# Two transformer blocks on one core: a pair's output kept in its own r and split later, the small projections' epilogue as a thread

## The reference

```
h  = rms_norm(x, attn_norm)
z  = h @ w_in                          # 2048 -> 1024 (pool) + 3*1024 (r, k, v) + 288 (rates)
zs = token_shift(z[1024:], mu)
r, k, v       = three parts of zs, 1024 each
zw, za, zg    = the last 288 of zs: 64, 64 and 160
decay         = exp(-exp(-softplus(-(w0 + tanh(zw) @ w_up)) - 0.5))
a             = sigmoid(a0 + za @ a_up)
g             = sigmoid(zg) @ g_up
y             = wkv7_scan(r, decay, k', v, -kk, kk*a)     # 16 heads of 64
y             = group_norm(y)*gn_g + gn_b + sum(r*k'*r_k)*v
rwkv_out      = y * g                                     # 1024
pool_out      = causal_multiscale_pool(z[:1024]) @ pool_w * pool_scale
x = x + concat(pool_out, rwkv_out) @ w_out
x = x + relu(rms_norm(x) @ w_ffn_up)^2 @ w_ffn_down
x = x + sigmoid(rms_norm(x) @ w_ple_gate) * (p @ w_ple_proj)
return rms_norm(x, final_norm)
```

## Time and profile before

| | |
|---|---|
| median of 3 runs | 3063.9 us |
| profiled execution, its own time | 3062.03 us |
| span from first to last instruction | 3060.2 us |
| mean granted TensorE clock | 0.975 of full speed |
| busy: PE, DVE, ACT, POOL | 96%, 63%, 47%, 6% of the span |
| DMA | 482.24 MB, 158 GB/s on average |

### The profile page before, as it was taken

One profiled execution on the slowest core, in us unless ns is written; L12 is line 12 of the kernel. 1 busy time (PEld: TensorE's weight loads), 2 busy tenths in 40 slices (PEclk: granted clock), 3 DMA queues, 4 the chain that ended last, 5 costly groups with the idle time before them and its releaser, 6 DMA issues.

```text
span 3060.2 us, 55785 instructions
## 1 busy us (share of the span) xinstructions
PE 2945.8 (96%) x23624; PEld 2874.8 (94%) x23624; DVE 1940.6 (63%) x2218; ACT 1445.7 (47%) x1815; POOL 192.8 (6%) x166
## 2 busy tenths in 40 slices
PE   7998999999999999999997999988899999999998
PEld 7987989999999999999997999976899999999997
DVE  6467767455666676677666676765656556555565
ACT  5356644444554444444445544543444444444464
POOL 0010011000000000000001020222000000000000
PEclk9998999999999999999999999987999999999999
DMA  6644523665566656655654534310366666666654
GB/s 208 187 120 127 166 72 95 183 185 173 187 179 187 186 177 187 183 177 180 191 182 125 176 110 132 103 57 7 95 187 184 183 183 184 182 185 182 184 169 142
DMA packets 252105, 482.24 MB, mean 158 GB/s; under 512 B 16944, under 2 KB 22320, under 8 KB 251728
## 3 DMA queue, kind: packets, MB, share of 16 engines
q1 hardware_dynamic: 251856, 478.68, 52.6%
HBM read 476.53 MB, written 2.10 MB: 156 GB/s over the span
## 4 chain that ended last, share of the span: by engine, by line
PE 83%; DVE 8%; ACT 5%; DMA 2%; issue 2%; POOL 0%; DVEq 0%; ACTq 0%; SPq 0%
PE psm L411 75%; PE psb L468 7%; DVE slo L325 3%; DVE ar L496 2%; ACT ar L493 2%; ACT shi L315 1%; DVE ar L504 1%; DMA raw<-in_w_in 1%; PE psb L476 0%; DVE x L496 0%; DVE ar L507 0%; ACT L493 0%; DMA raw<-in_w_down 0%; ACT gf L493 0%; DVE gl L504 0%
## 5 line engine op out<-in xcount | busy, mean ns | idle before, releaser
L325 DVE TENSOR_TENSOR slo<-raw,shi 128x1024 fp32r<-128x1024 f32 (+1 forms) x901 | 1125.0, 1254 | 715.8 <-ACT shi L315 713.2
L315 ACT ACTIVATE shi<-raw 128x1024 fp32r<-128x1024 f32 (+1 forms) x901 | 947.0, 1054 | 1174.4 <-PE psm L411 942.5
L411 PE MATMUL psm<-gh,shi 128*128 128x256 f32 x3664 | 1052.1, 287 | 17.1 <-DVE slo L325 14.6
L411 PE MATMUL psm<-gl,shi 128*128 128x256 f32 x3664 | 1040.9, 284 | 0.0
L411 PE MATMUL psm<-gh,slo 128*128 128x256 f32 x3664 | 1040.7, 284 | 0.0
L411 PE MATMUL psm<-hh,shi 128*128 128x256 f32 x3408 | 975.6, 286 | 24.0 <-DVE slo L325 17.0
L411 PE MATMUL psm<-hl,shi 128*128 128x256 f32 x3408 | 968.3, 284 | 0.0
L411 PE MATMUL psm<-hh,slo 128*128 128x256 f32 x3408 | 967.9, 284 | 0.0
L411 PEld LDWEIGHTS psm<-gh,shi 128*128 128x128 f32 x3664 | 706.6, 193 | 24.4 <-DVE slo L325 16.1
L411 PEld LDWEIGHTS psm<-gl,shi 128*128 128x128 f32 x3664 | 706.5, 193 | 1.0 <-issue 0.3
L411 PEld LDWEIGHTS psm<-gh,slo 128*128 128x128 f32 x3664 | 705.9, 193 | 0.3
(11 more groups left out here) (188 smaller groups left out, 1304.9 us busy)
## 6 DMA issues: line engine op xcount, KB each, us to landing
raw<-in_w_in SPq DMA_DIRECT2D x240, 512.0 KB, 3.7
raw<-in_w_up SPq DMA_DIRECT2D x176, 512.0 KB, 4.2
raw<-in_w_ffn_up SPq DMA_DIRECT2D x128, 512.0 KB, 3.8
raw<-in_w_ffn_down SPq DMA_DIRECT2D x128, 512.0 KB, 4.0
raw<-in_w_down SPq DMA_DIRECT2D x88, 512.0 KB, 4.6
raw<-in_w_out SPq DMA_DIRECT2D x64, 512.0 KB, 4.1
raw<-in_w_ple_gate SPq DMA_DIRECT2D x32, 512.0 KB, 4.9
raw<-in_w_branch_b SPq DMA_DIRECT2D x16, 512.0 KB, 3.9
```

The costliest lines, as they stand in the source:

```text
L315: hi_tok[j] = A.do(lambda e: e.activation(shi[:, s, 0:m], raw[:, q, 0:m], ACT.Copy), landed, pe_tok.get(j - NS), chain=False, cost=0.22 + ...
L325: lo_tok[j] = V.do(lambda e: e.tensor_tensor(slo[:, s, 0:m], raw[:, q, 0:m], shi[:, s, 0:m].bitcast(F), ALU.subtract), landed, hi_tok[j], ...
L411: e.matmul(out, l, r, start=st, stop=sp, skip_group_check=True),
```

## The change

First, a pair's output `y` is written over its own r (`zr[:, c, :]`, no longer read by then), `s.te` is set there, and the wait for `rkv_end` with the split into `hh`/`hl` goes into a generator of its own, `give`: put in lane 2 when `rkv_end` isn't there yet, run at once when it is. Second, the lora epilogue becomes a generator `lora` in lane 2 behind `finish`, with `scale_x` behind it; it frees its PSUM slot itself, so `group` now waits at a group's first tile until the slot has been freed, and the `rkv` epilogue waits until `lora` is written out.

```diff
--- before.py
+++ after.py
@@ -424,6 +424,8 @@
             k = 0
             for ti, (w, r, kc, c, n) in enumerate(ts):
                 j = cur[1]
+                if ti == 0:
+                    bg_until(lambda: slot.free is not None)
                 first_toks = (lo_tok[j], *(slot.free if ti == 0 else ()))
                 bg_ready(max(Queue.when(t) for t in first_toks))
                 PE.wait(*first_toks)
@@ -1389,7 +1391,6 @@
                 yield (tv,)
 
         nm1, x_done = nm, []
-        bgs[2].append(scale_x())
 
 
         al = Al()
@@ -1476,23 +1477,32 @@
         z_toks = {}
         l_tok = []
 
-        def epi_lora(ps, tp):
-            fg_drain()
-            need_rb()
+        def lora(ps, tp, slot):
+            while hn[0].rb is None:
+                yield
+            yield (hn[0].rb, tp)
             parts = [(lo_[0:n, i, :], lraw[0:n, i, :], 24 + i, n) for i, n in enumerate((128, 128, 32))]
             for dst, src, c, n in parts:
                 t_free = tt(src, ps[0:n, 256 * (c - 24):256 * (c - 24) + 256], rb[0:n, :], ALU.mult, tp)
+            slot.free = (t_free,)
             for dst, src, c, n in parts:
                 ta = act(dst, src, ACT.Copy, t_free, scale=omu[0:n, c:c + 1])
+            yield (ta,)
             for dst, src, c, n in parts:
                 tv = stt(dst[:, 1:256], src[:, 0:255], W("mu", c, 1)[0:n, :], dst[:, 1:256], ALU.mult, ALU.add, ta)
+            yield (tv,)
             act(lo_[0:64, 0, :], lo_[0:64, 0, :], ACT.Tanh, tv)
             act(lo_[:, 1, :], lo_[:, 1, :], ACT.Tanh, scale=0.5)
             ta = act(lo_[0:32, 2, :], lo_[0:32, 2, :], ACT.Tanh, scale=0.5)
+            yield (ta,)
             ts(lo_[:, 1, :], lo_[:, 1, :], 0.5, 0.5, ALU.mult, ALU.add, ta)
             l_tok.append(ts(lo_[0:32, 2, :], lo_[0:32, 2, :], 0.5, 0.5, ALU.mult, ALU.add))
             l_tok.append(ta)
-            return (t_free,)
+            yield ()
+
+        def epi_lora(ps, tp):
+            fg_drain()
+            bgs[2] += [lora(ps, tp, slots[nb[0] % 2]), scale_x()]
 
         group("lora", act_h, epi_lora)
 
@@ -1511,6 +1521,7 @@
 
             def epi(ps, tp):
                 fg_drain()
+                bg_until(lambda: l_tok)
                 if h:
                     bg_until(lambda: 3 in pooled and 0 in kk_tok)
                 tv = in_rms(rraw, ps, tp, kk_pe.get(0))
@@ -1728,11 +1739,21 @@
             tv = stt(yb, b.ap[:, 0:256], W("gn_g", c, 1), t2, ALU.mult, ALU.mult)
             b.free = (tv,)
             stt(yb, yb, W("gn_b", c, 1), bon, ALU.add, ALU.add)
-            tv = tt(yb, yb, gate_, ALU.mult, t_gate)
+            y = zr[:, c, :]
+            tv = tt(y, yb, gate_, ALU.mult, t_gate)
+            s.te = (tv,)
+            out = give(c, y, tv)
+            if rkv_end:
+                next(out)
+            else:
+                bgs[2].append(out)
+            yield ()
+
+        def give(c, y, tv):
+
             while not rkv_end:
                 yield
-            rw_tok[c] = hilo(hh[:, 8 + c, :], hl[:, 8 + c, :], yb, tv, rkv_end[0])
-            s.te = (rw_tok[c],)
+            rw_tok[c] = hilo(hh[:, 8 + c, :], hl[:, 8 + c, :], y, tv, rkv_end[0])
             yield ()
 
         for h in range(2):
```

## The result

The changed kernel took 3030.1 us (median of 4 runs, 3028.5 to 3033.9), the kernel before 3066.0 us on the same chip (4 runs, 3063.2 to 3069.0): a ratio of 0.988, with a 95% interval of 0.987 to 0.990, some 36 us less. Forecast were 3023 us, with 3006 to 3046 as the range. The profiled execution's span fell from 3060.2 to 3026.7 us, by 33.5 us.

A forecast was written before the change was run, and what follows sets the result against it. TensorE was taken to lose time waiting for a lora split and where the pairs' dependent chains stand alone. From 3062.0 us profiled, 27.5 for the pairs and 13 for lora gave 3021.5; plus 1.9, 3023 us; range 3006 to 3046.

The forecast's parts named there:

- Lora: Lora and first rkv group: TensorE's 9.9 us wait for a split goes, 13 us saved, 9.9 as lower end.
- The last two rkv groups: Stretch taking in pairs 2 and 3 nearly whole: 54 to 97.5 us, 7 of it loss.
- Rival (2): Last two rkv groups: POOL operations hold up DVE's splits, costing 10 us, total 3033; chance 0.08.
- Half 0's out2b: Only starts of pairs 6 and 7 stand beside its groups: 70 to 39 us.
- the loss of 7 us: Half 0's out2b: 7 us taken as lost, since only starts of pairs 6 and 7 stand there.
- Rival (1): Starts keep their price: out2b loses 20 us again, rkv groups 12, total 3041; chance 0.17, worst form 0.03.
- Out2a: Out2a with the rest of pairs 2 and 3, and pairs 4 and 5: 95 to 100 us, 6 lost.
- The tail: From half 0's out2b's fourth group's close to the next group's: 108 to 63 us, bounds 56 and 71.
- 60 - 7 + 2 + 8.7: Tail: old G-to-last-lower-part time, less full-clock saving, plus transposes and scaling, plus next group's close: 63 us.
- the saving of 7 us on G: Tail's beginning: 32 G products take 7 us at full clock instead of 14 at half.
- Rival (3): Pairs' part gives nothing, moved work costing the rkv groups what it saves behind; lora alone, 3051; chance 0.05.
- rival (4): TensorE falls to half clock over the last two rkv groups; at two thirds of it, 3076; chance 0.04.

The follow-up runs named there:

- the first experiment: Kernel before with only the lora epilogue moved to its own thread, pairs unchanged: 3053.6 us, ratio 0.9973.
- the split rows: Changed kernel with half 1's four out2b groups of 512 rows cut in two sets of four, 256 rows each: 3034.4 us, ratio 0.9908.
- the fill: Changed kernel plus 48 weight products whose result nobody reads, behind the G steps of pairs 6 and 7: 3034.6 us, ratio 0.991.
- the pairs' part alone: Kernel before with only the pairs' output written over r, lane released at once and split later, lora as before: 3043.1 us, ratio 0.9933.
- turns: Changed kernel with the G steps of pairs 6 and 7 taking turns: 3032.4 us, ratio 0.9886.
- turns with the split apart: Changed kernel with G steps taking turns and the split of a pair's output always its own step in the third lane: 3034.0 us, ratio 0.989.
- second profile: Changed kernel run again unaltered, as the ruler for the runs beside it: 3031.6 us, ratio 0.9882.

## Why the prediction was right, and where its sizes were off

**Lora.** Right in place and size: 12.1 us for 13, and the first rkv group without the wait. It stands alone in the first experiment, with the same 47 us, though only 8.3 us of it reached that run's total.

**The last two rkv groups.** Right: 98.1 us for 97.5, and POOL, empty there before, busy for 20.09 us. Rival (2), that POOL holds up the splits, was priced at 10 us; TensorE waited for a split there twice, 1.0 us in all. Of 17 splits in that stretch the median is 1.218 us and the longest 1.655. The splits, then splits and POOL operations that meet, and one of POOL's alone (the first):

```profile
L325 DVE TENSOR_TENSOR slo<-raw,shi x17: 1210/1218/1655, 1835.8 to 1927.0; 128x1024 fp32r<-128x1024 f32 x17
...
1849.19 0.92 POOL L502 TENSOR_SCALAR ar<-ar,par 128x256 f32<-128x256 f32 x1 [56.30 <-DVE ar L498]
...
1865.35 1.22 DVE L325 TENSOR_TENSOR slo<-raw,shi 128x1024 fp32r<-128x1024 f32 x1
1865.53 1.82 POOL L502 TENSOR_SCALAR gf<-ar,par 128x256 f32<-128x256 f32 x1 [7.62 <-DVE ar L498]
...
1875.88 3.17 POOL L498 TENSOR_TENSOR ar<-ar,con 128x256 f32<-128x256 f32 x3
1876.89 1.66 DVE L325 TENSOR_TENSOR slo<-raw,shi 128x1024 fp32r<-128x1024 f32 x1
```

They did meet: five of the 17 overlap a POOL operation. Two began inside one and took 1.66 and 1.44 us (at 1876.89 and 1904.70), 0.7 us lost together. Three (1855.36, 1865.35, 1880.72) began ahead of POOL's next one and took 1.22 or 1.23; there POOL's operation was the longer one, as at 1865.53, where it took 1.82 us, after 0.92 alone. The Trainium skill's rule on the shared lock (SBUF, State Buffer, who interferes with whom) says that issue order decides who blocks, and these rows agree with it. So the prediction's "by it this rival's full 18 us would show on DVE" took the rule too far: a split waits only where POOL's operation began first, and more of the waiting was POOL's own, which was busy for 20.09 us where 18.2 were taken as the most.

**Half 0's out2b.** 4.0 us better than forecast (34.8 for 39): the loss of 7 us that I took for starts beside short groups is about 3. Rival (1), that starts keep the 20 us, fell.

**Out2a.** 4.3 us worse (a rise of 9.3 for 5). The granted clock is at half for 10.2 us there (6.8 before), in runs of G products of pairs 4 and 5. I gave it the loss of windows with two starts; it has two starts, two G runs and two inverses. How much of the 4.3 the clock took was not tried apart.

**The tail.** The mechanism is right, and the term was mis-sized by 6 us (69.0 for 63, inside the bounds of 56 and 71; its parts, 60 - 7 + 2 + 8.7, add up to 63.7). The step that failed is "As TensorE now comes out of out2b's products, I take full clock": of the saving of 7 us on G only 1.6 came (15.2 us for 16.7 up to the inverse's first level). The clock fell to half 4.5 us behind the last of those products, at the same place in both profiles of the changed kernel, and the 26 products behind it took 12.3 us instead of 5.7, 6.6 us more. The granted clock over the tail's first 15 us, which the prediction wanted near 1.0, was 0.54. That the time follows from the clock is the reading of those rows and of two other runs: with the split rows the same 36 records took 4.98 us at full clock, for 8.70 here, and with the fill a G step took 2.07 us at half and 1.16 at full clock. No run held everything else and changed the clock alone. How long the half clock lasts doesn't set the tail by itself, either: with the pairs' part alone it lasted 23.9 us, the same G records took 3.78 and 8.69 us, and the 6.8 us more, which lay over the inverse, left the tail at 69.4. The three runs that changed the order there (fill, turns, turns with the split apart) all changed the clock's stretch (10.24, 27.3 and 30.7 us) and none got below 69.

**The sum.** Forecast 40.5 us by the profile, 33.5 came: 8.5 us were lost on the tail (6.0), out2a (4.3), the rkv groups (1.3) and lora (0.9), net of out2b's 4.0, and 1.5 came back from stages that the change doesn't touch. That out2b and those stages made good 5.5 us of the 12.5 lost was not foreseen; so far the total's nearness to the forecast is luck. Rival (3), no gain from the pairs' part, is refuted by that part alone (-20.5 us); rival (4), half clock over the rkv groups, by 0.97 there.

**Open.** What makes the clock fall behind out2b; and 2 us at pair 6's start: ScalarE's three copies out of PSUM at 2075.45 stand behind a weight split that waited 2.05 us for its DMA, a tile that TensorE reaches only behind the tail. Neither was tried.

## What to carry to other kernels

When an epilogue's chain of small steps holds the engine that prepares the next group's operands, cut it into steps that the scheduler can lay between those preparations; look at the order on that engine, not at its busy share. When a dependent chain ends a stage alone, the gain is in what holds its start (here a buffer that a later step had to release), and it can be priced by the products that move beside dense work; work added beside the chain (the split rows), or products to fill, slowed it here by as much as they brought or more. Don't count on full clock for a chain's first products because dense work stands ahead of them: read the granted clock at every such place of the trace, and what the engine did just before.

## What the runs showed of the hardware

I had expected TensorE's granted clock to outlast the dense products. Where pair 6's G comes straight behind out2b, the clock was at half 4.3 to 5.2 us behind out2b's last dense product: at 2076.76 for 2072.22 in the changed kernel, 2075.52 for 2070.96 in its second profile, 2092.09 for 2087.81 (pairs alone), 2074.27 for 2069.73 (split rows), 2079.25 for 2074.89 (turns) and 2078.10 for 2072.90 (turns with the split apart). With the fill it was 6.6 us (2077.23 for 2070.66). In between TensorE ran some 14 to 34 records, the pairs' and the fill's, and stood idle once, for 1.5 to 3.3 us, just ahead of the fall or across it. In the kernel before, where 130 records of pairs 4 and 5 come first, the clock fell 20.2 us behind (2090.05 for 2069.87). Which of this makes it fall isn't shown. The stretch lasted 17.07 us in both profiles of the changed kernel, 23.9 us with the pairs alone, and 27.3 and 30.7 us in the two runs with turns. In such a stretch a float32 product of 128 columns took 0.47 us, against 0.22 at full clock. Where a split of a weight tile on DVE and a POOL operation overlapped, the one that began second took longer (1.66 us for 1.22, 1.82 for 0.92). Two table loads more (32 for 30 on ScalarE's main line, 41.1 us for 38.5) cost nothing that the stages show.
